# A two-block transformer kernel: first block's projections moved forward, its attention done by pairs of heads between pieces of the convolution's products

## The reference, cut to what matters

```python
z = rmsnorm(x) @ w_in                      # 256 q-rank, 256 kv-rank, 32 k-rope, 3 x 512 conv columns
q  = (rmsnorm(z_q)  @ w_uq ).reshape(S, 8, 64 + 32)      # 8 heads: 64 plain + 32 rotated columns
kv = (rmsnorm(z_kv) @ w_ukv).reshape(S, 8, 64 + 64)      # plain key columns, values
k_rope = rope(z_k_rope)                    # 32 columns, the same for every head
s = (q_plain @ k_plain.T + rope(q_rot) @ k_rope.T) * 96 ** -0.5   # causal, softmax
a = softmax(s) @ v
c = b_gate * conv3(c_gate * xv)            # causal convolution of 3 taps over the tokens
x = x + rmsnorm(concat(rmsnorm(a), rmsnorm(c)) @ w_out)
```

## Time and profile before

| what | value |
|---|---|
| median of 3 runs | 2088.22 us (2083.9 to 2088.61) |
| profiled execution | 2085.66 us, its span 2083.8 us |
| PE busy | 2010.0 us, 96% of the span |
| DVE, ACT, POOL busy | 945.3, 774.1, 939.0 us |
| mean granted PE clock | 0.986 of full |

### The profile page before, as it was taken

How to read it: one execution, slowest core, us unless ns; L and a number is a source line. 1 busy time by engine, 2 the same in 40 slices (tenths; PEclk the granted TensorE clock), 3 DMA queues, 4 the chain that set the end, 5 groups by cost and what they waited for, 6 DMA issues and landing times.

```text
span 2083.8 us, 24712 instructions
## 1 busy us (share of the span) xinstructions
PE 2010.0 (96%) x9646; PEld 1675.3 (80%) x9646; DVE 945.3 (45%) x1421; ACT 774.1 (37%) x1116; POOL 939.0 (45%) x680
## 2 busy tenths in 40 slices
PE   6987989999997999999999999999999999999997
PEld 5777768888885798989897888888888888888886
DVE  5577373333225754545455322314566674132233
ACT  6246452232233433324244322323356554233232
POOL 4440344555454535353535544545533335454452
PEclk9999999999998999999999999999999999999998
DMA  5330127557322322222222333233322222233321
GB/s 159 99 116 21 55 69 106 120 92 116 101 81 81 101 81 81 81 82 80 90 71 81 101 101 101 81 100 101 115 86 80 80 81 91 91 101 101 101 87 54
DMA packets 170015, 188.56 MB, mean 90 GB/s; under 512 B 4168, under 2 KB 158544, under 8 KB 169808
## 3 DMA queue, kind: packets, MB, share of 16 engines
q1 hardware_dynamic: 167648, 182.07, 27.3%
q10 hardware_dynamic: 1904, 4.59, 4.4%
q0 software_dynamic: 384, 0.81, 0.2%
HBM read 180.77 MB, written 4.72 MB: 89 GB/s over the span
## 4 chain that ended last, share of the span: by engine, by line
PE 71%; issue 15%; POOL 9%; DVE 2%; ACT 2%; DMA 0%; SPq 0%; POOLq 0%; ACTq 0%; DVEq 0%
PE ps L627 23%; PE ps L628 22%; PE ps L629 22%; POOL w_lo L597 9%; PE ps L986 1%; PE ps L999 1%; PE ps L1013 0%; PE ps L1012 0%; DVE hn_lo L1663 0%; PE ps L662 0%; DMA o_buf<-in_x 0%; DVE scr L1638 0%; DVE x L1999 0%; DVE hn_lo L2004 0%; ACT w_hi L1090 0%
## 5 line engine op out<-in xcount | busy, mean ns | idle before, releaser
L597 POOL TENSOR_TENSOR w_lo<-raw,w_hi 128x512 fp32r<-128x512 f32 x652 | 920.7, 1443 | 1099.7 <-ACT w_hi L1090 1099.7
L627 PE MATMUL ps<-hn_hi,w_hi 128*128 128x512 f32 x1528 | 610.4, 399 | 24.5 <-DVE hn_lo L1663 9.7
L629 PE MATMUL ps<-hn_hi,w_lo 128*128 128x512 f32 x1528 | 599.3, 392 | 0.0
L628 PE MATMUL ps<-hn_lo,w_hi 128*128 128x512 f32 x1528 | 598.9, 392 | 0.0
L1090 ACT ACTIVATE w_hi<-raw 128x2048 fp32r<-128x2048 f32 x163 | 312.3, 1916 | 766.7 <-PE ps L629 759.1
L627 PEld LDWEIGHTS ps<-hn_hi,w_hi 128*128 128x128 f32 x1528 | 289.2, 189 | 99.4 <-issue 22.0
L627 PE MATMUL ps<-hid_hi,w_hi 128*128 128x512 f32 x888 | 348.5, 392 | 3.3 <-DVE hid_lo L2119 1.4
L628 PE MATMUL ps<-hid_lo,w_hi 128*128 128x512 f32 x888 | 345.7, 389 | 0.0
L629 PE MATMUL ps<-hid_hi,w_lo 128*128 128x512 f32 x888 | 345.6, 389 | 0.0
L628 PEld LDWEIGHTS ps<-hn_lo,w_hi 128*128 128x128 f32 x1528 | 289.6, 190 | 62.2 <-issue 3.8
L629 PEld LDWEIGHTS ps<-hn_hi,w_lo 128*128 128x128 f32 x1528 | 289.1, 189 | 61.6
(11 more groups left out here) (252 smaller groups left out, 1933.6 us busy)
## 6 DMA issues: line engine op xcount, KB each, us to landing
raw<-in_mlp_w SPq DMA_DIRECT2D x64, 1024.0 KB, 5.2
raw<-in_ret_w_in SPq DMA_DIRECT2D x24, 1024.0 KB, 5.2
raw<-in_att_w_in SPq DMA_DIRECT2D x12, 1024.0 KB, 5.2
raw<-in_w_gate SPq DMA_DIRECT2D x11, 1024.0 KB, 5.3
raw<-in_w_up SPq DMA_DIRECT2D x11, 1024.0 KB, 5.4
raw<-in_w_in SPq DMA_DIRECT2D x8, 1024.0 KB, 5.6
raw<-in_w_down SPq DMA_DIRECT2D x8, 1024.0 KB, 8.4
raw<-in_ret_w_out SPq DMA_DIRECT2D x8, 1024.0 KB, 5.0
```

The source lines that it names most:

```text
L597: ins = pool.tensor_tensor(w_lo[:, slot, at], raw[:, slot, at], w_hi[:, slot, at].bitcast(F32), ALU.subtract)
L627: pe.matmul(o, hi, rhs_hi, start=start, stop=False, skip_group_check=True)
L628: pe.matmul(o, hi, rhs_lo, start=False, stop=False, skip_group_check=True)
L629: return pe.matmul(o, lo, rhs_hi, start=False, stop=stop, skip_group_check=True)
```

## The change

The products of the first block stand in a new order: MIX keeps 3 chunks (q-rank, kv-rank, gate c of the first half), then UKV and UQ, and the other five convolution chunks are a phase CONVS of 20 quarters. The first attention uses the paired scheme of the second one, five quarters to a pair, and lies between the quarters. The score of a pair is now two products added in PSUM: three passes of 64 plain rows and three of 32 rotated rows, each for two heads. The rotated query rows stay where the projection left them (four heads on four groups of 32 partitions), and the rotated key rows are copied by six DMAs of 64 KB to the other three groups. The 16 copies of `spread_heads` are gone. `r` (the inverse norm) is applied to u once, squared, by POOL, and the first tap is on ACT. The group of gate c is emptied by ACT (`conv_gate`), no longer by DVE.

```diff
-MIX = Phase(None, [1] * 8)
+MIX = Phase(None, [1] * 3)
 UKV = Phase(MIX, [4])
 UQ = Phase(UKV, [4])
-WOUT = Phase(UQ, [1] * 4)
+CONVS = Phase(UQ, [1] * 5)
+WOUT = Phase(CONVS, [1] * 4)
...
+ONE_QUARTERS = 4 * CONVS.chunks
+ONE_EVERY = 5
...
+        class OnePair(Pair):
+            name, scale, negated = "one", DQ ** -0.5, (5, 8)
+            def qk(self, b):
+                h = 2 * self.p + b
+                r, q, k = self.rows(b), self.p, 4 + self.p
+                q_hi, q_lo = probs_t[r, q, :], Q_NOPE_LO[q][r, :]
+                nope = [(q_hi, hid_hi[r, k, :]), (q_hi, hid_lo[r, k, :]), (q_lo, hid_hi[r, k, :])]
+                r, q = slice(32 * (h % 4), 32 * (h % 4) + 32), 9 + h // 4
+                rope = [(hid_hi[r, q, :], hid_hi[r, 8, :]), (hid_hi[r, q, :], hid_lo[r, 8, :]),
+                        (hid_lo[r, q, :], hid_hi[r, 8, :])]
+                return nope + rope
...
 PE:
-            for n in (2, 3):
-                pe.wait_ge(pair_free[n % 2], UKV.group(n).freed(1))
-            pe.wait_ge(s["krep_done"], 32)
-            pe.wait_ge(s["q_rope_in"], 12 * 16)
-            pe.wait_ge(s["q_rope_lo_in"], 4 * 16)
...
-            attend(ATT1)
+            for quarter in range(ONE_QUARTERS + 2):
+                p, phase = divmod(quarter - 1, ONE_EVERY)
+                if phase == 0 and p:
+                    pair_values(ONES[p - 1], 1)
+                if phase == 0 and 0 <= p < ONE_PAIRS:
...
+                    pair_scores(ONES[p], (3,))
+                if phase == 1:
+                    pair_scores(ONES[p], (2, 0, 1))
+                if phase == 3:
+                    pair_transposes(ONES[p], 0)
+                if phase == 4 and p >= 0:
...
+                    pair_values(ONES[p], 0)
+                    pair_transposes(ONES[p], 1)
+                if quarter < ONE_QUARTERS:
...
+                    product(CONVS.chunk(n), CONVS.group(n), KD, 256, 0, hn_hi, hn_lo, None, ks, quarter % 4 == 0,
+                            quarter % 4 == 3)
+            stat(N_CONVG)
...
 ACT:
+            split_parts(UKV.chunk(0), ukv_parts())
+            for t in range(2):
+                hi_tile(N_Q, t, hid_hi[:, t, :])
+            rsqrt(N_KV, KV_RANK)
+            for t in range(2):
+                hi_tile(N_KV, t, hid_hi[:, 2 + t, :])
+            act.wait_ge(s["krope"], 4)
+            act.activation(hid_hi[0:32, 8, :], aux[0:32, 0, :], ACT.Copy).then_inc(s["krope_hi"], 1)
+            act.wait_ge(s["krope_hi"], 1)
+            act.wait_ge(s["krope_lo"], 1)
+            for ap in (hid_hi[:, 8, :].bitcast(F32), hid_lo[:, 8, :].bitcast(F32)):
+                for n in range(1, 4):
+                    act.dma_start(ap[32 * n:32 * n + 32, :], ap[0:32, :]).then_inc(s["krep_done"], 16)
...
+            conv_gate(0, MIX.group(2))
+            split_parts(UQ.chunk(0), uq_parts())
...
+                if quarter and quarter % 4 == 0:
+                    n = quarter // 4 + 1
+                    split(CONVS.chunk(n) if n < CONVS.chunks else WOUT.chunk(n - CONVS.chunks))
+                if quarter == 12:
+                    conv_gate(1, CONVS.group(2))
+                if quarter in (5, 17):
+                    conv_first_tap(quarter // 12)
+            act.wait_ge(s["conv_out"], 4)
+            act.wait_ge(s["one_t"], 8 * ONE_PAIRS)
+            for t in range(4):
+                square(N_CONVG, t, conv_u[t])
+            pair_shift(ONES[3], 1)
             rsqrt(N_CONVG, CONV)
...
 DVE:
+                if phase == 3:
+                    pair_prob_lo(a, 0)
+                    pair_probabilities(a, 1)
+                if quarter == 20:
+                    conv_closed(1)
...
+                if phase == 4 and quarter:
+                    pair_prob_lo(a, 1)
+                    pair_sum(a, 0)
+                if quarter in (4, 16):
+                    conv_opened(quarter // 16)
+                if quarter in (6, 18):
+                    conv_taps(quarter // 18)
+                if quarter == 8:
+                    conv_closed(0)
+            all_sums(N_CONVG)
+            pair_sum(ONES[3], 1)
             low(N_CONVG, lambda t: ("conv_group_norm", t), lambda t: o_buf[:, 4 + t, :], hn, 4)
```

More of the change, by code:

```diff
@@ L717, in _ @@
             ins.then_inc(s["kr_done"], 1)
[L718 to L722, removed]
-                if n == 3:
-                    stat(N_KV)
+            chunk_ready(MIX.chunk(2))
+            product(MIX.chunk(2), MIX.group(2), KD, 256, 0, hn_hi, hn_lo, stat_at(N_KV, 2))
             c = UKV.chunk(0)
@@ L763, in _ @@
                 ins.then_inc(s["group_done"], 1)
-                if n == 0:
-                    stat(N_CONVG)
-            def scores(a, h):
-                g = UQ.group(2 + h // 4)
-                pe.wait_ge(pair_free[g.pair], g.freed(h % 4 // 2))
-                for t, bank_read in Q_ORDER:
-                    if not a.first(h):
-                        pe.wait_ge(s["att_mx"], h * 4 - 4 + bank_read)
-                    for n, (q, k) in enumerate(a.qk(h)):
-                        ins = pe.matmul(a.score_ps(t), q[:, t * P:(t + 1) * P], k[:, 0:(t + 1) * P],
-                                        start=(n == 0), stop=(n == 2), skip_group_check=True)
-                    ins.then_inc(s["att_s"], 1)
@@ L1218, in _ @@
                 for m in range(2):
[L1219 to L1225 removed]
+                    act.activation(hid_hi[:, 4 + 2 * n + m, :], ps[:, g.bank(m), :], ACT.Copy).then_inc(s["kv_hi"], 1)
             for n in range(2):
@@ new lines, in pair_prob_hi, with pair_shift @@
+            def pair_prob_hi(a, b):
+                if a.p or b:
+                    act.wait_ge(a.sem("pv"), 2 * a.p + b)
+                for j, done in T_ORDER[b]:
+                    act.wait_ge(a.sem("t"), 8 * a.p + 4 * b + done)
+                    act.activation(a.pt(0, j), a.trans_ps(b, j), ACT.Copy).then_inc(a.sem("hi"), 1)
+            def pair_shift(a, b):
+                act.wait_ge(a.sem("pv"), 2 * a.p + b + 1)
+                if a.p:
+                    act.wait_ge(a.sem("o"), 2 * a.p - 1 + b)
+                here, there = a.rows(b), a.rows(1 - b)
+                act.activation(o_shift[here, :], a.out_ps(b)[there, :], ACT.Copy).then_inc(a.sem("shift"), 1)
@@ L1904, in _ @@
-            dve.wait_ge(s["mask_in"], 16)
-            attend(ATT1)
-            dve.wait_ge(s["att_pv"], H1)
+            for n in range(2):
+                g = UQ.group(2 + n)
+                for m in range(2):
+                    tile = 2 * n + m
+                    dve.wait_ge(s["q_nope_hi"], tile + 1)
+                    dve.tensor_tensor(Q_NOPE_LO[tile], ps[:, g.bank(m), :], probs_t[:, tile, :].bitcast(F32),
+                                      ALU.subtract).then_inc(pair_free[g.pair], 1)
```

670 lines of the change are left out of this document (289 added, 381 removed).

## The result

| | us | |
|---|---|---|
| before | 2085.57 | median of 10 runs (2082.81 to 2088.61) |
| after | 2092.61 | median of 10 runs (2090.03 to 2095.27) |
| after / before | 1.0032 | 95% interval 1.0022 to 1.0042 |

The change makes the kernel 7 us (0.3%) slower. The forecast was 2.6 us faster, and 2085.6 us; no run of the changed kernel was that fast, though 2092.61 lies inside the stated range of 2077.5 to 2094.

What follows compares the result with a forecast made beforehand. PE bound the front, one head's latency through four engines the first attention. WOUT 3.5 us earlier, less 0.9 of clock, gave 2.6 off 2085.66: 2083.1 profiled; with the median 2.6 higher, 2085.6 us, range 2077.5 to 2094.

Steps and rivals of the forecast that it cites:

- The stop at UKV: At UKV's first group, PE waits 8.0 us (5.5 to 10) for ACT's copy of gate c, queued behind the rotated keys.
- The clock behind it: After PE's wait at UKV, low clock costs 1.8 us, with 6 kept as upper end.
- PE's work for a pair: First attention: scores, values and transposes of two heads take PE 10.4 us, against 10.3 before.
- A change of rows: In the score passes, switching PE between matmuls of 128, 64 and 32 rows costs 0.2 us, ten times a pair.
- rivals 1 and 2: Score passes: either the six 64/32 changes a pair are free (2080.8 us, 28%) or 32-row passes run serially (2093.0, 14%).
- rival 3: Behind the stops at UKV and the tail, PE stays at 1.2 GHz for 12.5 us, 4.4 more each: 2094.4 us; 12%.
- rival 2: Score passes: the two heads' 32-row passes go one after the other, 7.4 us more: 2093.0 us; 14%.
- What is late next is ACT at quarter 12: In the quarters, ACT's weight rounding and gate c copy between exponentials and transposed probabilities cost 1.0 us (0 to 2.5).
- the tail, 15.5 us: From quarter 19's end to WOUT's first matmul, 15.5 us (12 to 19), of which PE works 4.6.
- PE reaches UKV at 64.8: At the front, PE gets through k-rope, chunk 2 and two sums to UKV's first matmul at 64.8 us.
- The bet on direction: Whole kernel: probability 0.31 of faster by over 0.3%, 0.56 of same, 0.13 of slower by over 0.3%.
- the trade of 23 us gained against 22.6 paid: Some 23 us of waiting and low clock removed; 9.8 at the front, 1.0 in the middle, 11.8 at the tail added.

Runs made afterwards that it cites:

- e1: Changed kernel with ACT copying the first half's gate c before the rotated keys, whose six DMAs are issued later; 2086.27 us.
- e2: Changed kernel with POOL holding the lo parts of CONVS chunks 3 and 4 until DVE's second-head divisions of pairs 1 and 2; 2086.33 us.
- e4: Changed kernel with three tiles' score passes grouped, all 64-row before all 32-row, six row changes a pair for ten; scores wrong, timing only; 2091.44 us.
- e3: Changed kernel with ACT's rounding of CONVS chunk 3 moved to quarter 9 and chunk 4's ahead of quarter 12's exponentials; 2086.85 us.
- e8: Changed kernel with POOL holding UKV's lo parts until DVE has summed kv-rank's squares; 2092.23 us.
- e9: Changed kernel with only POOL held, at four places: UKV's lo parts, CONVS chunks 3 and 4, WOUT's chunk 1; 2086.00 us.
- e5: Changed kernel with ACT rounding WOUT's chunk 1 earlier and POOL holding its lo parts until DVE has summed the convolution's squares; 2092.04 us.
- e6: Changed kernel with WOUT chunk 1 rounded earlier, POOL held behind the convolution's sums, and the convolution's chain put ahead of the last head's; 2086.58 us.

## Why the prediction was wrong

**Right, by its own steps.** The stop at UKV: 8.0 us forecast, 7.56 found, released by ACT's copy of gate c behind six DMA issues of 0.63, and e1 removes it. That its length came out so close is in part luck: both ends were late, PE by 1.8 us and the copy by 1.3. The clock behind it: 1.8 us forecast; 4.0 us at 0.50 cost 2.0 (6.0 us in e2's execution), and it came back under dense work, not after 12.5 us. PE's work for a pair: from 101.66 to 125.84 us five quarters (13.75) and pair 0 take 24.18, so 10.43 against 10.4. A change of rows costs 0.17 between 64 and 32 (e4), near the 0.2 of the forecast. (Without any price on changes the four pairs would be 8.0 us cheaper by the forecast's own count of ten; its 4.8 is the six 64/32 ones.) The 32-row passes of two heads overlap like the 64-row ones. So rivals 1 and 2 fall, and rival 3 in the form given. That the time lies 0.4 us from rival 2's 2093.0 is chance.

**Wrong: "What is late next is ACT at quarter 12 ... I put 1.0 us on it (0 to 2.5)".** This is the step that failed. What was late next was DVE, and because of POOL: waits of 2.98 and 1.59 us, of which e2 leaves 0.4; with one of 0.32 that e2 leaves too it is 4.9 in all. ACT's rounding, on which the 1.0 stood, was worth nothing measurable (e2 against e3). The step counted DVE's and ACT's work (12 us in a pair's 24) as if each engine ran at its own pace, and so put POOL beside DVE at nothing. In the old attention POOL was busy for only 5 us, and in the new middle for 33 of 98.8. This overlap is what the change brings with it, and the text had the clue: at the front it noted a step of 1.61 us "that takes 0.68", with POOL subtracting, priced it there, and did not carry it to the quarters and the tail.

**Wrong: the tail, 15.5 us, whose sums were taken as 3.5 us from the squares' start**. POOL is idle beside those sums. The three sums took 4.18 us for 2.28: 1.9 of the 2.4 that the tail is longer.

**Wrong: "PE reaches UKV at 64.8".** It was 66.6, by the wait of 1.66 us for a sum that was late beside POOL (e8). That POOL rests during the rotation held (4.96 us there for 5.3 forecast); that it works beside q-rank's tiles ten microseconds earlier was left out.

Together: 1.7 at the front, 3.9 in the middle (4.9 of waiting less the 1.0 forecast) and 1.9 at the tail are 7.5 of the 9.4 us by which WOUT was late. Of the rest, 0.6 us is a wait at the first quarter for the last plain query tile, and 0.9 is PE's own work in the quarters (93.9 us busy for 93.0). At the tail the sum over partitions ran at 1.2 GHz (2.08 us for 1.02, where 0.4 more was forecast). e9 shows the sum as a whole: POOL's starting times alone are worth 6.6 us of the 9.6, with two collisions moved and not removed.

The Trainium skill, SBUF — State Buffer, "Who interferes with whom", has the rule that I had not used: a VectorE instruction with two SBUF inputs contends with a GpSimd instruction that reads SBUF, and one in a two-port mode contends with GpSimd too; whichever comes second waits for the other's whole instruction. One with at most one SBUF input, outside those modes, does not contend. The traces agree: 1.28 to 4.43 us for four divisions, 1.42 to 3.44 for two normed tiles, POOL's four subtractions from 5.06 to 6.30 beside the sums, and 1.35 unchanged for DVE's subtractions from PSUM.

The bet on direction failed for the same reason: the trade of 23 us gained against 22.6 paid left no room, and the uncounted stretches all fell on one side, since the chains at the front and at the tail have PE waiting at their end.

## What to carry to other kernels

When work is interleaved to fill PE, list not only each engine's busy time but which of DVE's instructions have all their operands in SBUF, and where POOL will run beside them; hold POOL until they are through if its result is not yet due. Holding it only moves the collision if the chain has more such instructions behind, so look where it lands. The order of the queues at the seams (gate c behind six DMA issues, the convolution's chain behind the last head's) and POOL beside DVE cost more here than the interleaving gained: with the same interleaving and both mended, the kernel goes from 2092.6 to 2069.2 us, 16 us faster than before.

## What the runs showed of the hardware

- Beside POOL's subtractions of 128x512 (5.03 us for four, undisturbed, in e2), a DVE instruction whose tensors all lie in SBUF was held up by 0.6 to 1.0 us, about as much for a small one as for a large one: four divisions of 128 to 512 columns 4.43 us for 1.28, two normed tiles of 512 columns 3.44 for 1.42, three sums 4.18 for 2.28. POOL was held up as well where DVE had two such inputs, 6.30 and 6.33 us for four (tail and front of after), but not beside the divisions (5.06). DVE's subtractions with one operand in PSUM and POOL's beside them kept their time.
- Behind a stop of 7.6 us PE ran at 1.2 GHz for 4.0 us in after's execution and 6.0 in e2's. Behind one of 3.0 us it did so in some executions (e1, e4, e5) and not in others (after, e6, e8). In e1's it cost 1.6 us by WOUT. Each kernel has one trace, so how much of the scatter between executions of one kernel comes from this is not shown.
- The issue of a DMA of 64 KB held ACT's queue for 0.63 us, six of them for 3.8 us.
